# RWKV scan: the next tile's 16x16 inverses placed earlier in VectorE's order

## The reference, cut to what matters

```
def step(state, inp):
    r_t, w_t, k_t, v_t, kk_t, a_t = inp
    sk = einsum('bhvk,bhk->bhv', state, kk_t)
    state = state * w_t - sk[..., None] * (kk_t * a_t) + v_t[..., None] * k_t
    return state, einsum('bhvk,bhk->bhv', state, r_t)
```

## Time and profile before

| | |
|---|---|
| time, median of 3 runs | 3805.52 us (3795.18 to 3812.78) |
| profiled execution: its own time | 3805.52 us |
| profiled execution: span of the instructions | 3803.7 us |
| TensorE busy (mean granted clock 0.968) | 3520.6 us, 93% of the span |
| VectorE busy | 1869.2 us, 49% |
| ScalarE busy | 1152.0 us, 30% |
| GpSimd busy | 865.4 us, 23% |
| `rwkv_scan`, first tile's inverse to the last tile's `make_u` | about 3218 to 3545 us of the span |

### The profile page before, as it was taken

How to read it: one execution, slowest core, us unless ns; L and a number is a source line. 1 busy time by engine, 2 the same in 40 slices (tenths; PEclk the granted TensorE clock), 3 DMA queues, 4 the chain that set the end, 5 groups by cost and what they waited for, 6 DMA issues and landing times. The chain is left out here.

```text
span 3803.7 us, 64572 instructions
## 1 busy us (share of the span) xinstructions
PE 3520.6 (93%) x27290; PEld 2019.6 (53%) x27290; DVE 1869.2 (49%) x2911; ACT 1152.0 (30%) x2214; POOL 865.4 (23%) x544
## 2 busy tenths in 40 slices
PE   8999999989988999989899998999899996888898
PEld 3448864445545565644346446544444344877543
DVE  3336662323217777832446327422757874655322
ACT  1127751112224444411321107312213442221124
POOL 0000013430000000034333220233115751333532
PEclk9999999999989999999999999999899998989999
DMA  6000023334255555450331102110155444533400
GB/s 243 22 23 2 2 73 106 111 79 144 75 145 135 136 136 135 113 189 22 138 122 56 34 0 90 67 44 11 63 225 187 154 173 118 163 105 89 161 11 39
DMA packets 312534, 374.65 MB, mean 98 GB/s; under 512 B 161588, under 2 KB 211236, under 8 KB 309558
## 3 DMA queue, kind: packets, MB, share of 16 engines
q1 hardware_dynamic: 312248, 370.52, 31.4%
HBM read 271.90 MB, written 98.29 MB: 97 GB/s over the span
## 5 line engine op out<-in xcount | busy, mean ns | idle before, releaser
L2192 DVE TENSOR_SCALAR_CACHE_REDUCE la_s<-psum 128x1280 f32<-128x1280 f32 x128 | 191.0, 1492 | 122.9 <-PE psum L2229 122.9
L2161 ACT ACTIVATE la_s<-la_s,la_negm 128x1280 f32<-128x1280 f32 x128 | 175.5, 1371 | 220.6 <-DVE la_s L2192 220.6
L970 POOL TENSOR_TENSOR lg_seven_s<-other_columns 128x512 f32<-128x512 f32 x4 | 5.1, 1264 | 827.8 <-POOLq L112 807.3
L991 PE MATMUL psum<-room,x_rows 128*128 128x512 f32 x320 | 145.4, 597 | 6.8 <-POOL x_rows L970 6.8
L970 POOL TENSOR_TENSOR wg_seven_s<-other_columns 128x512 f32<-128x512 f32 x5 | 6.3, 1267 | 591.6 <-POOLq L112 543.8
L835 DVE CUSTOM_DVE_ANT_0 wa_s<-psum,window_mask_rows 128x640 f32<-128x640 f32 (+1 forms) x128 | 100.6, 786 | 71.6 <-PE psum L890 71.6
L3309 POOL TENSOR_TENSOR x_rows<-x_rows,pg_g 128x512 f32<-128x512 f32 x56 | 84.0, 1500 | 153.6 <-DVE pg_g L3458 139.9
L793 ACT ACTIVATE wa_s<-wa_s,wa_negm 128x640 f32<-128x640 f32 (+2 forms) x160 | 117.3, 742 | 0.9 <-DVE wa_negm L838 0.9
L991 PE MATMUL psum<-rp_t,rp_seven_s 128*128 128x512 f32 x256 | 117.0, 600 | 0.0
L991 PE MATMUL psum<-room,rp_seven_s 128*128 128x512 f32 x256 | 115.2, 593 | 1.6 <-DVE rp_seven_p L1040 1.6
L2229 PE MATMUL psum<-first_weights,latent_qr 32*128 32x320 f32 x1024 | 101.1, 447 | 5.7 <-issue 5.7
(11 more groups left out here) (719 smaller groups left out, 7914.0 us busy)
## 6 DMA issues: line engine op xcount, KB each, us to landing
la_v<-latent_v SPq DMA_DIRECT2D x64, 320.0 KB, 10.0
x_rows<-rwkv_raw SPq DMA_DIRECT2D x40, 512.0 KB, 4.7
room<-rwkv_raw SPq DMA_DIRECT2D x33, 512.0 KB, 4.7
later_slot<-in_ada_w_dram SPq DMA_DIRECT2D x16, 1024.0 KB
rwkv_raw<-x_rows SPq DMA_DIRECT2D x64, 256.0 KB, 2.9
rwkv_raw<-x_rows SPq DMA_DIRECT2D x32, 512.0 KB, 3.9
room<-in_odd_w_in_dram SPq DMA_DIRECT2D x6, 2048.0 KB, 12.7
la_k<-latent_kT SPq DMA_DIRECT2D x32, 320.0 KB, 5.6
```

What stands on the lines that cost most here:

```text
L991: last = pe.matmul(bank, left[:, k, :], right[:, k, :], start=fresh and k == 0, stop=k == HK - 1, skip_group_check=True)
L2161: act.activation(s, s, ACT.Exp, scale=-1.0, bias=negm[:, u % RING:u % RING + 1], accum_out=total[:, head(u) % 2, tile(u):tile(u) + 1]).the ...
L2192: dve.tensor_scalar(by_lane(s_sb[:, u % RING, :]), by_lane(s_banks)[:, :, 0:SPAN], -SCALE, FAR, ALU.mult, ALU.min, accum_out=negm[:, u % R ...
```

## The change

VectorE's order at the end of each tile, and nothing else. `small_first` of the next tile stands ahead of the first `make_u`, and `small_last` stands between the first `make_u` and the first `state`; before, they stood behind the first `state` and behind the second `make_u`.

```diff
-                    make_u(i, 0)
-                    state(i, 0)
                     if i + 1 < NT:
                         steps = small_steps_of(i + 1)
                         small_first(i + 1, steps)
-                    make_u(i, 1)
+                    make_u(i, 0)
                     if i + 1 < NT:
                         small_last(i + 1, steps)
+                    state(i, 0)
+                    make_u(i, 1)
                     state(i, 1)
```

## The result

The changed kernel takes 3808.31 us in the median (3800.84 to 3822.19, 22 runs) beside 3802.57 us (3791.08 to 3812.78, 22 runs) for the kernel before: ratio 1.0021 [1.0013, 1.0029]. That is about 8 us slower (0.0021 x 3803; the medians lie 5.7 us apart), where 23 us were forecast. Its profiled execution took 3804.03 us around a span of 3802.2 us.

What follows compares the result with a forecast made beforehand. Taken as bound: one chain through TensorE and VectorE in each tile, without slack. Delay 38.4, less 16.3 coming back, plus 1 for the clock, gave +23 us: 3829 us (3815 to 3840; 8 in 10: 3801 to 3843).

Steps and rivals of the forecast that it cites:

- Tile 0: Scan's first tile: `small_first` waits for the corners of tile 1, so U starts 5.1 us late.
- `small_first` in tiles 1 to 6: In front of U: GpSimd's output instructions hold VectorE's small ones; U starts at GpSimd's end + 2.3 us.
- `small_last` ahead of the first `state`: Between U and `state`: takes 4.06 us; from U's start to chunk 1's products 6.86 us.
- What comes back: Ahead of the next inverse: TensorE's 18.9 us wait for the transfers goes; VectorE can use 16.3 us.
- The clock: TensorE's restarts after idling, about 1 us each: about five fewer before the inverse, six more before chunk 1; +1 us.
- GpSimd did not give way: Rival: GpSimd gives way or small operands don't collide, so `small_first` fits the idle slot; 3801 us; chance 0.17.
- the clock did not stay low to the tile's end: Rival: TensorE's lower clock level holds to the tile's end, another 2 us a tile; 3843 us; chance 0.11.
- the wait for the transfers did not stay: Rival: the eight transfers before the inverse are late for another reason, nothing comes back; 3845 us; chance 0.05.
- I am wrong if: Refutation: small instructions keep 0.13 to 0.27 us while GpSimd runs, or the wait for the transfers is still there.

Runs made afterwards that it cites:

- experiments 2: GpSimd's seven scan output instructions cut from 1024 to 64 columns: in the changed kernel 3791.73 us, 0.9978; in the kernel before 3802.76 us, 1.0011.
- 5: Kernel before, in tiles 1 to 6 `small_first` ahead of the first U and GpSimd's last three output instructions waiting for that U: 3795.98 us, 0.9993.

## Why the prediction was right or wrong

The sign was right and the size was not: +8 us instead of +23, in the two profiles 7.7 instead of 23.1, so 15.4 us less. By its own steps:

- *Tile 0*: 5.1 forecast, 4.9 measured. Right, for the reason given.
- *`small_first` in tiles 1 to 6*: the hold by GpSimd is what happens, and experiments 2 and 5 show it from both sides. J to U grew by 26.9 us in these tiles (31.8 less 4.9). The size was a little off: U comes 1.59 us behind GpSimd's end, not 2.3, since seven of the 15 instructions were through by then, and the eighth ended with it, and not three to five.
- *`small_last` ahead of the first `state`*: U to chunk 1's products was forecast at 6.86 us and measured at 6.59 to 6.64 in tiles 0 to 6. Right. With the steps above, chunk 1 comes 34.6 us late in sum (31.8 + 2.8), not 38.4: 3.8 of the miss.
- *What comes back*: TensorE's wait is gone whole, 18.9 us, and the chain of transfers did have its slack. Behind F 18.6 us came back where 10.3 were booked (16.3, less 6 for the clock): 8.3 of the miss. The clock has some 3 of these (next step). The other 5 lie within the 7.0 us by which this stretch differs between the two profiles of the kernel before (129.5 and 136.5), so no cause is read from them.
- *The clock*: **this is the step that failed.** It was +1, as -5 in front of the inverse and +6 in front of chunk 1. The five restarts in front of the inverse went (granted clock 0.50 to 0.65 before, 1.00 after). Of the six in front of chunk 1 two came, in tiles 3 and 6, at 1.4 us by tile 3 (17.71 - 16.34): about 3 us, an estimate, instead of 6. Taking the 1.62 us of idling in tile 6 of the earlier trace rows as a rule for every such idle was the mistake. It did not even hold for the kernel before, whose second profile has the same products behind the same idle time at 1.15 us:

```profile
3505.64 1.15 PE L4905 MATMUL psum<-rs_S,rs_HmT 64*64 64x64 f32 x32 [1.62 <-DVE rs_S L4739]
```

- *A term that the sum put at nothing*: TensorE's waits for instruction loads behind SP's large loads, which the change shifts out of the inverse, from 5.0 us to 0.4. With them the inverse gave back 8.3 us where the clock's 5 were booked: 3.3 of the miss. The view of waits showed them as "issue", and I read past them.

Why the clock falls behind one idle time and not behind another of the same length no run was made to tell.

None of the rivals held. GpSimd did not give way (1.76 us for an instruction of 16 elements), the clock did not stay low to the tile's end (in tile 6, where it was low for longest, the granted clock is 1.00 from 3507 to 3513), and the wait for the transfers did not stay. "I am wrong if" named the first and the third. What failed was a sum of large terms with opposite signs, of which the delay was off by a tenth. That all its misses fell to the same side is in part luck, and its bounds for the clock (-5 to +8) held nothing for the "issue" waits.

## What to carry to other kernels

A slot in which VectorE idles is free for work on SBUF operands only if GpSimd is idle in it too: look at what GpSimd does in the slot before moving VectorE's work there, or hold GpSimd back, which restored U here (without a gain in time that these runs show). When a change moves a wait, ask what was timed by that wait; here it set when three large loads met TensorE's instruction loads. One row is no rule: before a price is multiplied by six, look for the same idle time with another outcome. And if the last thing on the path is a queue that issues eight transfers, issue half of them elsewhere first: here that gained 0.4%, where the reordering lost 0.2%.

## What was not expected of the hardware

- Instruction loads share the DMA engines with data. In 6 us with three 512-KB transfers the packets of data took 98.4% of the 16 engines' time and one instruction load 1.0%; TensorE then stood 1.45 us for nothing that the program waits for, until 1.25 us behind that load's end. Moving the transfers moved or removed such waits (5.0 us in the inverse before, 0.8 and none with the loads moved).
- A copy with one operand is held as well as a product of two: 1.19 us for 128x8, until GpSimd's instruction ended.
- GpSimd hardly notices these short instructions: its last three take 1.95, 2.37 and 2.38 us in tile 2 of the changed kernel, beside 1.90, 2.35 and 2.35 in that of the kernel before, where VectorE's small part runs behind them.
- The same idle time of TensorE came with either level of its clock. Behind 2.75 us in the changed kernel 32 products took 1.15 us in tile 2 and 1.97 in tile 3 (granted clock 1.00 and 0.62 over the 4 us that follow), and behind 1.62 us in tile 6 of the kernel before 1.97 us in one profile and 1.15 in the other.
